# Moving the lower weight copies and three activation buffers by 64 bytes in a two-block transformer kernel

## Time and profile before

| | |
|---|---|
| median of three runs | 2609.7 us (2608.3 to 2610.85) |
| time of the profiled execution | 2614.2 us |
| its span, first to last instruction | 2612.6 us |
| TensorE matmuls | 2548.0 us busy, 98% of the span, 13,872 of them |
| TensorE weight loads | 2133.6 us busy, 82% |
| VectorE | 1631.4 us busy, 62% |
| ScalarE | 964.2 us busy, 37% |
| GpSimd | 96.0 us busy, 4% |
| mean granted TensorE clock | 0.988 of full speed |
| chain of work that ended last | TensorE 93%, VectorE 4%, ScalarE 1%, DMA 1% |

### The profile page before, as it was taken

How to read it: one execution, slowest core, us unless ns; L and a number is a source line. 1 busy time by engine, 2 the same in 40 slices (tenths; PEclk the granted TensorE clock), 3 DMA queues, 4 the chain that set the end, 5 groups by cost and what they waited for, 6 DMA issues and landing times.

```text
span 2612.6 us, 36055 instructions
## 1 busy us (share of the span) xinstructions
PE 2548.0 (98%) x13872; PEld 2133.6 (82%) x13872; DVE 1631.4 (62%) x2569; ACT 964.2 (37%) x1425; POOL 96.0 (4%) x185
## 2 busy tenths in 40 slices
PE   7999999999999999999999999999999899999997
PEld 4888888888888887669888888888888788888886
DVE  6777557754546557666655566676666876644447
ACT  4334533121212244763332243353222454533224
POOL 0000000000000000000000000000001000000000
PEclk8999999999999999999999999999999999999998
DMA  6332223433333321002645453234445422222222
GB/s 259 131 113 97 78 85 128 155 112 106 112 112 130 106 73 49 1 2 75 199 148 174 169 185 109 82 120 155 163 157 192 139 101 81 81 97 91 95 97 89
DMA packets 82937, 303.66 MB, mean 116 GB/s; under 512 B 9200, under 2 KB 11376, under 8 KB 81520
## 3 DMA queue, kind: packets, MB, share of 16 engines
q1 hardware_dynamic: 56736, 206.82, 23.2%
q0 software_dynamic: 26064, 94.91, 10.8%
HBM read 299.60 MB, written 2.10 MB: 115 GB/s over the span
## 4 chain that ended last, share of the span: by engine, by line
PE 93%; DVE 4%; ACT 1%; DMA 1%; issue 1%; SPq 0%; DVEq 0%; ACTq 0%
PE G L500 20%; PE G L501 20%; PE G L502 20%; PE G L527 5%; PE G L528 5%; PE G L529 5%; PE B L1030 2%; PE G L586 1%; PE G L587 1%; PE G L588 1%; PE G L992 1%; DVE Wlo L1718 1%; PE B L1006 1%; PE G L673 1%; PE G L675 1%
## 5 line engine op out<-in xcount | busy, mean ns | idle before, releaser
L1146 ACT ACTIVATE Whi<-Wraw 128x1024 fp32r<-128x1024 f32 x357 | 375.0, 1052 | 452.7 <-DMA Wraw<-wstream_dram 434.0
L1718 DVE TENSOR_TENSOR Wlo<-Wraw,Whi 128x1024 fp32r<-128x1024 f32 x357 | 436.1, 1222 | 130.3 <-ACT Whi L1146 129.4
L500 PE MATMUL G<-h_hi,Whi 128*128 128x512 f32 (+1 forms) x1024 | 361.7, 353 | 0.3 <-ACT T L1245 0.3
L501 PE MATMUL G<-h_lo,Whi 128*128 128x512 f32 (+1 forms) x1024 | 359.4, 351 | 0.0
L502 PE MATMUL G<-h_hi,Wlo 128*128 128x512 f32 (+1 forms) x1024 | 357.7, 349 | 0.0
L500 PE MATMUL G<-hs_hi,Whi 128*128 128x512 f32 x720 | 287.4, 399 | 4.0 <-DVE Wlo L1718 4.0
L502 PE MATMUL G<-hs_hi,Wlo 128*128 128x512 f32 x720 | 283.8, 394 | 0.0
L501 PE MATMUL G<-hs_lo,Whi 128*128 128x512 f32 x720 | 282.6, 392 | 0.0
L501 PE MATMUL G<-hid_lo,Whi 128*128 128x512 f32 (+1 forms) x760 | 278.9, 367 | 0.0
L500 PE MATMUL G<-hid_hi,Whi 128*128 128x512 f32 (+1 forms) x760 | 278.8, 367 | 0.0
L502 PE MATMUL G<-hid_hi,Wlo 128*128 128x512 f32 (+1 forms) x760 | 277.3, 365 | 0.0
(11 more groups left out here) (484 smaller groups left out, 4585.2 us busy)
## 6 DMA issues: line engine op xcount, KB each, us to landing
Wraw<-wstream_dram SPq DMA_DIRECT2D x357, 512.0 KB, 3.3
Araw<-adaw_dram POOLq DMA_DIRECT2D x180, 512.0 KB, 3.8
FIRST<-firstw_dram SPq DMA_DIRECT2D x6, 1024.0 KB, 21.9
X<-xin_dram SPq DMA_DIRECT2D x4, 1536.0 KB, 11.3
out_dram<-X SPq DMA_DIRECT2D x16, 128.0 KB, 1.7
ROW<-rows_dram SPq DMA_DIRECT2D x2, 768.0 KB, 7.1
CB<-cvec_dram SPq DMA_DIRECT2D x2, 512.0 KB, 10.8
CB<-cvec_dram POOLq DMA_DIRECT2D x1, 512.0 KB, 4.9
```

Source lines behind the costliest of these rows:

```text
L500: pe.matmul(o, wh, hi[:, a:b], start=(k == 0), stop=False)
L501: pe.matmul(o, wh, lo[:, a:b], start=False, stop=False)
L1146: act.activation(Whi[:, t % 4, :], Wraw[:, t % 4, :], ACT.Copy).then_inc(w_hi, 1)
L1718: dve.tensor_tensor(Wlo[:, t % 4, :], Wraw[:, t % 4, :], Whi[:, t % 4, :].bitcast(F32), ALU.subtract).then_inc(w_lo, 1)
```

## The change

Three unused buffers are added. `Wlo_line` (64 bytes in each partition) stands ahead of `Wraw` and `Wlo`, `Whi_line` (64 bytes) ahead of `Whi`, and `h0_line` (64 bytes) ahead of the stack that holds `h0` in one use and `mixa` and `mixb` in the other. No instruction is added, removed or moved.

```diff
         X = sb("X", [P, KD, NT])
+        sb("Wlo_line", [P, 16])
         ws = ExitStack()
         Wraw = sb("Wraw", [P, 4, D], where=ws)
         ws.close()
         Wlo = sb("Wlo", [P, 4, D], F32R)
+        sb("Whi_line", [P, 16])
         Whi = sb("Whi", [P, 4, D], F32R)
...
         SH = sb("SH", [P, NT], where=hyb)
+        sb("h0_line", [P, 16], where=hyb)
         p1 = ExitStack()
         h0 = [sb("h0_hi", [P, KD, NT], F32R, p1), sb("h0_lo", [P, KD, NT], F32R, p1)]
```

## The result

The changed kernel takes 2633.48 us, median of 6 runs (2625.76 to 2639.0), beside 2610.27 for the kernel before on the same chip (6 runs, 2606.57 to 2615.17). The ratio is 1.0089, with a 95% interval of 1.0072 to 1.0106: slower by 23 us, and 1.5 us above the top of the forecast range. The profiled execution took 2633.88 us.

What follows compares the result with a forecast made beforehand. TensorE's matmuls, busy for 98% of the span, were taken as the bound. Terms of -2.0, -0.4, +7.2, +1.0 and -4.3 gave +1.5 us on 2609.7, so 2611 us, range 2595 to 2632.

Steps and rivals of the forecast that it cites:

- Where the time could move: Whole kernel: only the spacing of TensorE's matmul starts, 13,872 matmuls, could change the sum; forecast +1.5 us.
- Leaving the other engines at nothing: Weight splits on ScalarE and VectorE and the loads: no change taken; 21 us if TensorE's cover went.
- the rival that the layout does nothing: All TensorE matmuls: distances cannot matter by the skill's rule, time stays 2609.7 us; chance 0.07.
- The odd/even rule: Source-to-weights distance in TensorE's matmuls: even multiples of 64 bytes run at 232.9 ns, odd ones at 228.9 at best.
- the mixes: Tiles on `mixa` and `mixb`: with `h0`, 744 matmuls of 512 columns go from 232.9 to 230.2 ns, -2.0 us.
- The mixture of paces: Every stage: two thirds of matmuls meet the odd case, one third the even, giving 230.2 ns; chance 0.33.
- The pair that the prediction named: TensorE's matmuls: the distance from one matmul's source to the next one's weights sets the pace, 232.9 or 228.9 ns.
- the bulk: First MLP to the second block's first layer: some 5,500 matmuls of 512 columns lose 1.3 ns each, +7.2 us.
- the last layer: Last layer's series: some 1,400 matmuls leave 233.3 ns for 230.2, -4.3 us.
- 256 columns: Matmuls of 256 columns: -0.4 us on `h0` and the mixes, +1.0 us for 3,200 in the bulk.
- Slower by long series in a slow rhythm: Second MLP and the layer behind it: long series settle at 233.3 ns, 2637 us; chance 0.20, spread over 2616 to 2637.
- The tell-tale: Second MLP's 240 us windows: a count falling from 1,051 to 1,030 would mean the slow rhythm has taken over.

Runs made afterwards that it cites:

- the series alone: Kernels computing nothing of the model: only TensorE, series of 96 matmuls at chosen operand placements; 226.67 ns per 512-column matmul with weights and sources level.
- the series of pairs: Kernel computing nothing of the model: two kinds of matmul alternate, each with its own weights and source; 228.3 to 236.7 ns in the placements told of.
- the second one of the same kernel: The kernel before, not one line changed, profiled once more: 2601.23 us, beside 2609.18 for the run next to it.
- the first execution: The kernel before, unchanged, in the profiled execution that the prediction read: 2614.2 us.

## Why the prediction was wrong, point by point

**Where the time could move: right.** The only terms that moved by microseconds are spacings of TensorE's matmuls. The splits stayed at 1052 and 1221 ns, and all that is not a 512- or 256-column matmul of a product came to +1.3 us of 19.7. Leaving the other engines at nothing was right, and so was rejecting the rival that the layout does nothing: the same instructions at other addresses took 0.9% more.

**The odd/even rule: wrong, and the first step that failed.** The prediction had distances of 64 and 128 bytes before it and read them as odd and even. The period is 256 bytes. Of the two odd distances 64 gives 228.9 and 192 gives 233.3; of the two even ones 0 gives 226.7 and 128 gives 232.2 to 233.3. The kernel before had only 64 and 128 of these four, and its rows could not tell a period of 128 from one of 256. It struck `h0`, moved to 192 bytes from `Whi`: the forecast took 230.2 ns and -2.0 us for it and the mixes, the trace has 231.5 and 232.9 ns in alternating tiles, and 0.0 us. With `h0` alone moved, where no mixture is in play, the time did not fall either.

**The mixture of paces: wrong, and the term that made the miss.** "I take the mixture, (2 x 228.9 + 232.9) / 3 = 230.2 ns" held that a block's three spacings each pay for their own pair. Its bracket, 228.9 to 233.3, was to hold the price from both sides. The rates measured in the first MLP with the attention, in the second MLP and the third layer are 234.3, 234.1 and 231.1 ns, two of them above the bracket, and the series alone gives 231.1, 233.9 and 234.3 for those distances. A series with unequal distances settles in a rhythm of its own, over several matmuls, and its mean is no mean over pairs. The pair that the prediction named, a source and the next matmul's weights, failed by itself too: level with the next weights gave 230.0 ns in the series of pairs, not 226.7. What had misled was the earlier trace rows, where the pace turns with the source within a tile: it shows that a rhythm can change within a few matmuls, not that each matmul has a price. In the sum: +7.2 for the bulk became +22.8 us, and -4.3 for the last layer became +1.0; with `h0` and the mixes at 0.0, 512 columns came to +23.6 us where +0.9 was forecast.

**The last layer: wrong in sign.** It was to leave 233.3 and gain; it went to 234.1. The gain rested on one execution: in the second one of the same kernel the layer ran at 228.9, and against that it lost 7.3 us. So the reading that distance alone does not set this layer's rate was right; that the entry into the series sets it was not shown.

**256 columns: small, and open in sign.** +0.6 us in all was forecast. Against the first execution -5.2 came, as the rates fell to 115.6 to 117.9 ns; against the second +2.7, since its first MLP ran at 113.6. The 3,200 of the sum are 2,856 by the trace, which moves it by 0.1 us. The series alone has 115.6 for the changed distances. What is good at 512 columns need not be at 256: level sources give the best rate at one (226.7) and the worst of the placements tried at the other (120.0).

**The rival that came nearest.** Slower by long series in a slow rhythm, 2637 us: its place was right (first and second MLP, and the layer behind them), the cause half right (whole series did run in a slow rhythm, but one of those that the new distances allow and not the old 233.3; that the entry sets it was not shown), and the price of 24 us at 512 columns near the 22.8 measured for these stages, though by other rates: 234 in place of 233.3 in the MLPs, and 231.1 in the third layer. The 2,637 took 2.6 us more at 256 columns, where the first execution shows 5.2 less. The tell-tale stood: 1,027 is under the 1,030 named for it. The chance for this side was too low because the upper bound had been taken from series with equal distances only.

**The range.** It ended at 2632 because the upper end of the slow case was left out as unlikely. How much slower the change looks depends on the record it is held against: 19.6 us of span against the first execution of the kernel before, 32.6 against the second, itself a run of 2601.23 us at the low end, 23.2 between the medians.

**The rule of the skill.** The Trainium skill, SBUF — State Buffer, "Who interferes with whom", gives TensorE two independent read ports, one for the moving operand and one for the weight load, and has it wait on no one. In the series alone no other engine works, the granted clock is 1.00, and the spacing still goes from 226.7 to 236.7 ns with the addresses of TensorE's own operands. Here the measurement decides. The runs show which distance costs what; they do not show which accesses meet, or where.

## What to carry to other kernels

Where TensorE's matmuls are back to back with a weight load beside each, count starts per stage, and look at the distance between moving operand and weights modulo 256 bytes: here level (or 252 bytes) was the best at 512 columns and 64 bytes next, while the unequal distances of this change cost 2 to 3.5% against level. Price a new layout by a short kernel of series that has exactly the distances, the widths and the order of the weights; don't interpolate between the rates of others. And look at a second record of the unchanged kernel before a stage's pace is ascribed to its operands or a gain is counted on it, since a series can have two rhythms.

## What the runs showed of the hardware

- With a 128 x 128 weight load beside each, float32r matmuls of 512 columns start every 226.67 to 236.67 ns at full clock, by the distances of their operands, with no other engine at work. The same at 256 columns: 113.3 to 120.0 ns.
- The spacings are periodic to the nanosecond of the records. 64 bytes gives 226, 229, 232 over and over, for whole tiles and layers; 128 bytes gives 229, 237, 230, 238; one rhythm at 192 bytes is 233, 233, 234.
- One placement can hold two rhythms: 231.1 and 234.3 ns for the changed kernel's distances, 230.0 and 233.3 at 48 bytes, 228.3 and 236.7 in the series of pairs. In the series the repeats differ in what ran just ahead, but each of these kernels was profiled once, and the unchanged kernel has two rhythms in its last layer (228.9 and 233.3 ns) and in its first MLP's 256 columns (113.6 and 117.7) from one execution to the next. So what chooses is not shown. A rhythm lasted for a whole layer in the kernel.
- Open: why 252 bytes is as good as level and 4 bytes as bad as any; which accesses meet; and what made the third layer take the rhythm of 231.1 ns and the MLPs that of 234. No run changed the entry into a series alone inside the kernel.
